# Two decoder blocks on one core: the hybrid layers' rotary halves turned by copies on ScalarE instead of a matmul on TensorE

## The reference

```python
def apply_rope(x, positions):
    ...
    ang = positions.astype(jnp.float32)[..., None] * inv_freq
    cos = jnp.cos(ang)[:, :, None, :]
    sin = jnp.sin(ang)[:, :, None, :]
    xf = x.astype(jnp.float32)
    x1, x2 = xf[..., :half], xf[..., half:]
    return jnp.concatenate([x1 * cos - x2 * sin, x2 * cos + x1 * sin], axis=-1).astype(x.dtype)

def hybrid_mixer(h, positions, w_in, b_fgate, w_fox_out, w_dsa_out, w_sb_out, w_out):
    proj = h @ w_in
    ...
    dq = apply_rope(dq, positions)
    dk = apply_rope(dk, positions)
    q_idx = apply_rope(idx_q.reshape(b, s, N_IDX_HEADS, IDX_DIM), positions)
    k_idx = apply_rope(idx_k.reshape(b, s, 1, IDX_DIM), positions)[:, :, 0]
    ...
```

## Time and profile before

| | |
|---|---|
| median of 3 runs | 2405.51 us (2404.97 to 2410.62) |
| the profiled execution | 2403.74 us, span 2401.9 us |
| mean granted clock of TensorE | 0.968 |
| TensorE matmuls busy | 2264.0 us, 94% |
| TensorE weight loads | 2157.3 us, 90% |
| VectorE | 1502.5 us, 63% |
| ScalarE | 1081.5 us, 45% |
| GpSimd | 350.4 us, 15% |
| HBM traffic | 155 GB/s over the span |

### The profile page before, as it was taken

The page is one execution under the profiler, slowest core; times in us unless marked ns, Lnnn a source line. Parts: engine busy times, 40 slices in busy tenths (PEclk is TensorE's granted clock), DMA queues, the critical chain, the costliest instruction groups (busy, mean ns, idle before and its releaser), DMA issues.

```text
span 2401.9 us, 40464 instructions
## 1 busy us (share of the span) xinstructions
PE 2264.0 (94%) x17516; PEld 2157.3 (90%) x17516; DVE 1502.5 (63%) x2186; ACT 1081.5 (45%) x1285; POOL 350.4 (15%) x300
## 2 busy tenths in 40 slices
PE   7988899998789999999999899999999999899998
PEld 6878799997679999999998798999999988788998
DVE  5566687843467878667756547667656556556665
ACT  4445544534455445335336355335334236445333
POOL 1680000045000000000535110000000015310000
PEclk9999999998899999999999799999999999989999
DMA  8663255543234554555643344455555643344552
GB/s 244 178 169 105 97 178 200 161 157 106 70 106 168 181 196 159 194 175 175 186 127 109 113 162 155 162 201 173 186 177 176 161 146 108 106 158 132 181 203 91
DMA packets 314660, 374.28 MB, mean 156 GB/s; under 512 B 23127, under 2 KB 280931, under 8 KB 313331
## 3 DMA queue, kind: packets, MB, share of 16 engines
q1 hardware_dynamic: 309283, 353.83, 45.5%
q0 software_dynamic: 3424, 11.50, 1.7%
q10 hardware_dynamic: 1776, 6.37, 0.8%
HBM read 362.49 MB, written 9.18 MB: 155 GB/s over the span
## 4 chain that ended last, share of the span: by engine, by line
PE 83%; DVE 9%; ACT 5%; issue 2%; POOL 0%; DMA 0%; ACTq 0%; DVEq 0%
PE banks L857 23%; PE banks L860 22%; PE banks L858 22%; PE banks L885 3%; PE banks L886 3%; PE banks L889 3%; DVE wlo L1752 2%; ACT whi L1335 2%; PE banks L1113 1%; PE banks L1151 1%; PE banks L1137 1%; PE banks L1033 1%; PE banks L1020 1%; DVE x_lo L1810 1%; PE banks L867 1%
## 5 line engine op out<-in xcount | busy, mean ns | idle before, releaser
L857 PE MATMUL banks<-x_hi,wlo 128*128 128x256 f32 (+1 forms) x4344 | 1110.0, 288 | 39.7 <-DVE wlo L1752 15.4
L858 PE MATMUL banks<-x_lo,whi 128*128 128x256 f32 (+1 forms) x4344 | 1098.5, 285 | 0.0
L1335 ACT ACTIVATE whi<-raw 128x2048 fp32r<-128x2048 f32 (+1 forms) x340 | 637.3, 1878 | 680.0 <-PE banks L860 617.6
L857 PEld LDWEIGHTS banks<-x_hi,wlo 128*128 128x128 f32 (+1 forms) x4344 | 843.6, 194 | 60.5 <-issue 34.2
L858 PEld LDWEIGHTS banks<-x_lo,whi 128*128 128x128 f32 (+1 forms) x4344 | 844.5, 194 | 1.0 <-issue 1.0
L1752 DVE TENSOR_TENSOR wlo<-raw,whi 128x2048 fp32r<-128x2048 f32 (+2 forms) x292 | 658.3, 2264 | 170.7 <-ACT whi L1335 170.4
L860 PE MATMUL banks<-x_hi,whi 128*128 128x256 f32 x4344 | 691.9, 285 | 0.0
L860 PEld LDWEIGHTS banks<-x_hi,whi 128*128 128x128 f32 x4344 | 599.6, 194 | 3.6 <-issue 0.9
L825 POOL TENSOR_TENSOR wlo<-raw,whi 128x512 fp32r<-128x512 f32 x184 | 239.7, 1340 | 1173.9 <-ACT whi L1335 1173.9
L885 PE MATMUL banks<-x_hi,wlo 128*128 128x256 f32 (+1 forms) x632 | 177.1, 312 | 31.5 <-DVE gt L1786 11.6
L886 PE MATMUL banks<-x_lo,whi 128*128 128x256 f32 (+1 forms) x632 | 169.1, 299 | 0.0
(11 more groups left out here) (254 smaller groups left out, 1966.3 us busy)
## 6 DMA issues: line engine op xcount, KB each, us to landing
raw<-in_ffn_w_gu SPq DMA_DIRECT2D x88, 1024.0 KB, 5.2
raw<-in_ffn_w_down SPq DMA_DIRECT2D x66, 1024.0 KB, 5.1
raw<-in_ffn_w_up SPq DMA_DIRECT2D x44, 1024.0 KB, 5.1
raw<-in_w_in SPq DMA_DIRECT2D x42, 1024.0 KB, 5.3
raw<-in_ca_w_kv SPq DMA_DIRECT2D x16, 1024.0 KB, 5.3
raw<-in_od_w_in SPq DMA_DIRECT2D x12, 1024.0 KB, 5.1
raw<-in_ev_w_in SPq DMA_DIRECT2D x10, 1024.0 KB, 6.2
raw<-in_w_in SPq DMA_DIRECT2D x20, 512.0 KB, 5.1
```

The lines of the kernel that those rows point to most:

```text
L857: eng.matmul(out, a[1], b[0], start=first and i == 0, stop=False, skip_group_check=True)
L858: eng.matmul(out, a[0], b[1], start=False, stop=False, skip_group_check=True)
L1335: eng.activation(whi[s % SETS][:, 0:ch["n"]], raw[i % SLOTS][:, 0:ch["n"]], ACT.Copy).then_inc(S["weights_hi"], 1)
```

## The change

The turned features are written by ScalarE into the scratch row where VectorE's product with the sine goes, by four copies per group, each from 32 partitions to 32 others, two of them with scale -1. TensorE's swap and its matrix are gone, and the table of constants is 128 columns narrower. VectorE's first product reads that scratch row and writes it in place, where before it read PSUM. ScalarE's group j stands in iteration 9 + j of its loop, behind the rounding of the chunk two units ahead.

```diff
-    out["swap_full"] = swap(32)
...
+        def turned_x(g, j):
+            return wk[:, 4 + j % 2, 0:g["n"] * SEQ].rearrange("p (n c) -> p n c", c=SEQ)
+
...
-            def turn_pairs(rope, j):
-
-                g, r0 = rope["groups"][j], rope["r0"]
-                eng.wait_ge(S["lin_free"], g["unit"]["taken"])
-                if j >= 2:
-                    eng.wait_ge(S["qk_rot_used"], r0 + j - 1)
-                x = ft[:, g["tile"]:g["tile"] + g["n"], :].rearrange("p n c -> p (n c)")
-                eng.matmul(rope_bank[j % 2][:, 0:g["n"] * SEQ], C("swap_full"), x, start=True, stop=True).then_inc(S["qk_roped"], 1)
-
...
-                    if rope and 0 <= i - rope["at"] < len(rope["groups"]):
-                        turn_pairs(rope, i - rope["at"])
...
+            def turn_pairs(rope, j):
+
+                g, r0 = rope["groups"][j], rope["r0"]
+                eng.wait_ge(S["lin_free"], g["unit"]["taken"])
+                if j >= 2:
+                    eng.wait_ge(S["qk_rot_used"], r0 + j - 1)
+                turned = turned_x(g, j)
+                for p0 in range(0, P, HD):
+                    for to, by, sign in ((p0, p0 + HD // 2, -1.0), (p0 + HD // 2, p0, 1.0)):
+                        m = eng.activation(turned[to:to + HD // 2], ft[by:by + HD // 2, g["tile"]:g["tile"] + g["n"], :], ACT.Copy, scale=sign)
+                m.then_inc(S["qk_roped"], 1)
+
...
+                    if st.get("rope") and 0 <= i - st["rope"]["at"] < len(st["rope"]["groups"]):
+                        turn_pairs(st["rope"], i - st["rope"]["at"])
...
-                by_sin = wk[:, 4 + j % 2, 0:n * SEQ].rearrange("p (n c) -> p n c", c=SEQ)
+                by_sin = turned_x(g, j)
...
-                step(eng.tensor_tensor(by_sin, rope_bank[j % 2][:, 0:n * SEQ].rearrange("p (n c) -> p n c", c=SEQ), ss, ALU.mult))
+                step(eng.tensor_tensor(by_sin, by_sin, ss, ALU.mult))
```

More of the change, by code:

```diff
@@ L974, in mem_sums @@
                 m.then_inc(S["mem_ss"], 1)
-            def turn_pairs(rope, j):
-                g, r0 = rope["groups"][j], rope["r0"]
-                eng.wait_ge(S["lin_free"], g["unit"]["taken"])
-                if j >= 2:
-                    eng.wait_ge(S["qk_rot_used"], r0 + j - 1)
-                x = ft[:, g["tile"]:g["tile"] + g["n"], :].rearrange("p n c -> p (n c)")
-                eng.matmul(rope_bank[j % 2][:, 0:g["n"] * SEQ], C("swap_full"), x, start=True, stop=True).then_inc(S["qk_roped"], 1)
             def linear(st):
-                nm, parts, units, rope = st["norm"], st["parts"], st["units"], st.get("rope")
+                nm, parts, units = st["norm"], st["parts"], st["units"]
                 for i, un in enumerate(units):
```

## The result

The changed kernel took 2387.34 us (median of 5 runs, 2384.64 to 2397.12) against 2406.03 us beside it (5 runs, 2404.97 to 2413.77). The ratio is 0.9937, interval 0.9919 to 0.9954: 15 us gained (11 to 19), where 9.5 were forecast.

A forecast was written before the change was run, and what follows sets the result against it. TensorE was taken to bound the kernel; 4.76 us of swaps per layer gave 9.5 us over two layers, less 0 for copies and 0 for VectorE, so 2396.0 us from the 2405.51 median, range 2390 to 2403.5.

The forecast's parts named there:

- TensorE bounds, and what it drops comes off: Hybrid input projection, both layers: TensorE, 100% busy, sets the pace, so removed swaps shorten each stage by 4.76 us.
- The price of a swap: TensorE, seven swaps per layer: 0.85 us per 512-column swap, 0.42 per 256-column one, 0.95 for the fifth.
- The copies: ScalarE, per layer: 2.2 us per wide group, 1.4 per narrow, 13.0 in all, hidden in its idle time.
- the 13 that were named as a sign: Sign of being right: ScalarE's idle time before its weight roundings falls by some 13 us per layer.
- The wait that the change adds: ScalarE waits for VectorE's rotation two groups before, worst at the sixth group; VectorE may stand 2 us, TensorE loses nothing.
- VectorE beside GpSimd: First layer: two-SBUF-operand products slow by 1.4 to 4.8 us, cost 0; rival loses 3 us plus 1.7 by clock, chance 0.07.
- the fifth swap at half its 1.91 us: Swap behind each layer's gate unit, at low clock: 0.95 us gained if the clock returns after the same time.
- The other way round: Clock rival's favourable side, low stretches at the gates shorter: 12.9 us gained; clock chance 0.12, of which 0.02 faster.
- the forecast's own 2392: Whole kernel: lower end of the forecast's own range, 2392 to 2399 us, with 11.4 us gained by a kinder clock.
- absorbed later: Rival, in attention: a wait that does not move with TensorE leaves 0 to 4 us gained, 2403.5; chance 0.09.
- the slower one: Rival: small copies make ScalarE the bound, weights late from 1.15 us per 512-element copy; at 1.5, 2412.7 us; chance 0.05.
- the swaps' price was not hidden: Answers the rival that other work already hides TensorE's price for the swaps, so removing them does nothing; chance 0.01.

The follow-up runs named there:

- the four profiled kernels with the whole change: The changed kernel, itself run again, it with the unused swap matrix kept, and it with ScalarE's copies written into PSUM; mean 2391.6 us over 23 runs.
- the repeat: The kernel before, run once more unchanged as a control against itself: 2406.23 us (10 runs), ratio 1.0004.

## Why the prediction was right, and where its size was off

**TensorE bounds, and what it drops comes off.** Right. It is 100% busy in both stretches, with no new wait, and at full clock the stages gave 9.4 us where the sum had 9.5.

**The price of a swap.** Right to 0.1 us: 4.7 and 4.8 us per stage at full clock for 4 x 0.85 + 3 x 0.42 = 4.7; the fifth alone 0.9 and 1.1; seven more of it 0.88 each. (The 2.88 us that the prediction reads between neighbouring units lie between the two output tiles of one unit; the differences, and so the prices, are the same.)

**The copies.** Dearer than taken, 2.56 and 1.70 us a group for 2.2 and 1.4, since they start 0.64 us apart, where the 128x512 ones at 1133.48 started 0.52 apart. That is 15.3 us per layer for 13.0, and hidden all the same (at full clock the stages are the same within 0.2 us without copies and with twice as many). The Trainium skill, ScalarE: Activation LUTs, "What ACT_TABLE_LOAD costs", gives 186 ns + 0.833 ns per element for an activation with immediate scale and bias. By this figure an estimate for 512 elements is 0.61 us; the trace's 0.63 agrees within 3%. The same section states that instructions in a row overlap by some 93 ns; these copies, 0.64 us from start to start, do not show it.

The idle time before the roundings fell by 31.5 us, not by the 13 that were named as a sign; its two stretches do not cover equal work. Over the equal work of the first stage ScalarE's idle time went from 41.0 to 19.7 us, 21.3 less: 15.0 us more of busy time and a stage that is 6.4 us shorter.

**The wait that the change adds.** Right, and milder than drawn: VectorE's fourth rotation let the sixth group go at 1189.39 instead of the 1192.25 taken from before, and the rounding behind it started at 1193.96 instead of 1196.6.

**VectorE beside GpSimd.** The effect came, but not where it was named: of the two wide products beside GpSimd one took 0.97 us and the other 0.68, no more than without it, and the two narrow ones took 1.52 and 1.50 us for 0.42. Over the layer that is 2.4 us, between the 1.4 and 4.8 of the prediction. Its cost of 0 was right, shown by the kernel with the operand in PSUM, and this rival falls.

**What the sum did not have: some 6 us more.** The prediction priced the fifth swap at half its 1.91 us and let the low stretches stay as they were, plus or minus 1.7 us per layer. "The other way round", 12.9 us gained, stood there without a chance of its own. Both profiles of before have 17.1 and 13.7 us of low clock at the gates in sum, the four profiled kernels with the whole change 10.2 each. That is 5.1 us less on average, half of it time: 2.6 us, so that the touched stages gave 9.4 + 2.6 = 12.0 us in these profiles. But this is not shown to be the doing of the change. The two other kernels without any swap, the one without copies and the one with each copy made twice, have 17.1 us (10.2 and 6.8), and so have both kernels in which a part of the swaps is left to TensorE, though these gained 4.6 us for a price of 1.7 and 11.5 for 7.6. The stretch at the gates differs by as much between two profiles of one kernel. The mechanism was right, but the size fell short by some 6 us: the result, 2390.4 us on the time of before, lies below the forecast's own 2392 and only 0.4 us inside the wider range, which was luck.

**What stays open.** Over all runs the four kernels with the whole change average 2391.6 us (23 runs), those of before 2407.0 (68 runs, the repeat among them): 15.4 us. 12.0 lie in the touched stages of the profiles, 3.4 outside, where both run the same instructions. Single profiles can't place them: these parts took 2282 and 2286 us in two profiles of before and 2276, 2276, 2285 and 2288 in four of the changed kind. The largest jump lies far ahead of the change, in the first block. The same stretch of work (between the same two roundings of weights) in the two profiles of before:
```profile
162.90:181.00 18.10, 16.40 (x118) 14.84 (x119) 14.23 (x49) 9.36 (x16) 12.84 (x11) 1.00 0.50 171
...
158.90:182.30 23.40, 17.77 (x118) 15.80 (x119) 17.15 (x52) 9.36 (x16) 14.19 (x12) 0.85 0.39 135
```
The changed kernel has the same two values, 18.1 in its first profile and 23.4 in its second. The first hybrid layer's attention took 129.4 and 125.5 us in the two profiles of before, 125.3 and 129.4 in those of after. So such jumps come and go in both kernels.

The mean granted clocks of all runs say a little more. An estimate from each run's span and mean clock: the kernel before stood at the low level for 168.0 us on average (63 runs), the whole change for 159.6 (23 runs). If half of the low time is lost, 4.2 us of the gain (0.7 to 7.7) come by the clock, and 11.1 (9.2 to 13.0) at full clock, where the swaps' price is 9.3. The kernel with the swaps moved to the end stood low for 148 us against 174 in the runs of before beside it. Half of that is 12.9 us (6.6 to 19.2), enough for all of its gain of 8.7. So this kernel gained by the clock and not by less work, by an estimate that needs the half for all of the low time. Whether the place of the swaps does it, how, and in which stage, was not shown.

The other rivals: no run shows a part of the gain absorbed later; the slower one needed between two and three times the copies; and the swaps' price was not hidden, since it is what the stages lost.

## What to carry to other kernels

Where one engine is busy for all of a stage, price a removed instruction by the distance between its neighbours with it and without it, and check the copies' engine for idle time between its own deadlines; that sum held to 0.1 us in the touched stages at full clock. Then ask for the clock in several profiles of the same kernel before comparing single ones: here equal instructions differed by up to 12 us, and four profiles agreed on a shorter low stretch that others with the same or fewer matmuls did not show. Before units are mixed, look at which buffers the mixed one must wait for.

## What the runs showed of the hardware

- ScalarE copies 32 partitions to 32 others in 0.64 us for 512 fp32 elements and 0.43 us for 256, start to start; a 128x512 one took 615 ns. Into PSUM the copy of 512 took 593 ns instead of 630.
- In the changed kernel's first layer the gate unit (14 columns) ran at the full level, and the low level came behind it (1184.0 to 1187.4), while 256-column matmuls ran. TensorE was busy all the time. In the first profile of before the low level began within the gate unit, at 1186.5 us. The changed kernel's timeline there, ahead of it the stretch up to the fall:
```profile
1174.00:1184.00 10.00, 10.00 (x89) 10.00 (x88) 7.20 (x8) 6.89 (x9) 9.92 (x9) 1.00 0.91 286
...
1182.95 1.04 PE L862 MATMUL banks<-whi,x_hi 128*128 128x14 f32 x8
1183.85 0.46 PE L859 MATMUL banks<-whi,x_lo 128*128 128x256 f32 x1
1184.11 0.41 PE L860 MATMUL banks<-wlo,x_hi 128*128 128x256 f32 x1
...
1188.43 0.28 PE L860 MATMUL banks<-wlo,x_hi 128*128 128x256 f32 x1
```
- With the 14-column matmuls in turn with 256-column ones, and TensorE idle for 4.2 and 3.9 us just before, the clock stood at 0.50 for 23.9 us in each layer; with the units apart and no such wait it was 3.4 to 10.2.
- With the copies made three times TensorE waited 6.7 and 6.6 us in the first layer, and a second low stretch of 6.8 us began during the second wait, at 1210.8 us.
- A VectorE product of two SBUF operands of 256 elements took 0.42 us with GpSimd idle and 1.52 and 1.50 us beside it; of 512 elements 0.69 us with GpSimd idle, 0.68 and 0.97 beside it. With one operand in PSUM the 256 elements took 0.42 us beside it too.
